# Row pairs in flight and attention weight pieces kept for both token halves: a change to a two-block transformer kernel

## The reference, cut to what matters

```python
for i in range(DEPTH):                      # DEPTH = 2
    h = x * scale + shift
    f = short_conv_mixer(h, ...) if i % 2 == 0 else diff_attention(h, w_qkv, ...)
    x = layer_norm(ALPHA * x + gate * f, ...)
    h = x * scale + shift
    f = peer_ffn(h, w_q[i], sub_keys[i], u[i], v[i])
    x = layer_norm(ALPHA * x + gate * f, ...)
```

```python
act = gelu(einsum('td,thkd->thk', xc, u[idx]))
out = einsum('thk,thkd->td', g * act, v[idx])
```

## Time and profile before

| | us |
|---|---|
| runs (3) | median 2861.89, 2859.72 to 2866.51 |
| the profiled execution | 2860.44 |
| its span, first to last instruction | 2858.7 |
| TensorE busy | 2556.7 (89%) |
| VectorE busy | 1577.9 (55%) |
| ScalarE busy | 630.5 (22%) |
| POOL busy | 674.2 (24%) |
| mean rate of the transfers | 329 GB/s |
| mean granted TensorE clock | 0.982 |

### The profile page before, as it was taken

One profiled execution on the slowest core, in us unless ns is written; L12 is line 12 of the kernel. 1 busy time (PEld: TensorE's weight loads), 2 busy tenths in 40 slices (PEclk: granted clock), 3 DMA queues, 4 the chain that ended last, 5 costly groups with the idle time before them and its releaser, 6 DMA issues.

```text
span 2858.7 us, 26727 instructions
## 1 busy us (share of the span) xinstructions
PE 2556.7 (89%) x9887; PEld 1591.7 (56%) x9887; DVE 1577.9 (55%) x3459; ACT 630.5 (22%) x1826; POOL 674.2 (24%) x687
## 2 busy tenths in 40 slices
PE   7999989999999899999889877999878999777776
PEld 6874548856884578758555422655525646322222
DVE  4562135524551546533768885365795565974544
ACT  1001211001000120000223333342333533332222
POOL 1110000100010001100234454243353243544332
PEclk9999999999999999999999999999999999999999
DMA  9894426845793448856789999999999999999997
GB/s 384 343 362 152 186 79 258 352 180 199 294 356 119 191 170 335 314 189 261 273 340 421 421 421 421 418 413 421 420 420 399 411 422 421 421 410 421 421 421 313
DMA packets 121128, 941.46 MB, mean 329 GB/s; under 512 B 14845, under 2 KB 16277, under 8 KB 19494
## 3 DMA queue, kind: packets, MB, share of 16 engines
q0 software_dynamic: 93344, 669.09, 57.8%
q1 hardware_dynamic: 27654, 270.66, 24.0%
HBM read 938.65 MB, written 1.05 MB: 329 GB/s over the span
## 4 chain that ended last, share of the span: by engine, by line
PE 62%; DMA 22%; DVE 9%; ACT 3%; issue 1%; SPq 1%; POOL 1%; DVEq 0%; POOLq 0%
PE psW L917 19%; DMA ring<-in_peer_uv_dram,lamt 19%; PE psF L1257 11%; PE psF L856 11%; DVE ring L2439 4%; PE psW L1358 3%; DMA mring<-in_tail_w_dram 2%; PE psW L826 2%; PE psW L796 2%; PE psW L1276 2%; PE psW L785 2%; PE psF L892 1%; POOL ring L630 1%; PE psF L1173 1%; PE psW L837 1%
## 5 line engine op out<-in xcount | busy, mean ns | idle before, releaser
L1257 PE MATMUL psF<-ring,p_diag 128*128 128x512 f32 x2048 | 959.5, 614 | 226.9 <-ACT p_diag L1663 226.6
L2439 DVE SCALAR_TENSOR_TENSOR ring<-ring,h 128x1024 f32<-128x1024 f32 x512 | 620.8, 1224 | 435.3 <-DMA ring<-in_peer_uv_dram,lamt 432.0
L630 POOL DMA_INDIRECT ring<-in_peer_uv_dram,lamt x512 | 585.4, 1143 | 1017.2 <-PE psF L1257 819.6
L1257 PEld LDWEIGHTS psF<-ring,p_diag 128*128 128x128 f32 x2048 | 380.6, 194 | 749.2 <-issue 391.4
L917 PE MATMUL psW<-hT,ring 128*128 128x256 f32 x2560 | 558.4, 380 | 1.9 <-DMA ring<-in_gu_t_dram 1.9
L917 PEld LDWEIGHTS psW<-hT,ring 128*128 128x128 f32 x2560 | 487.3, 190 | 77.5 <-issue 10.0
L856 PE MATMUL psF<-ring,arena 128*128 128x512 f32 x704 | 304.2, 593 | 3.2 <-DVE arena L2098 3.0
L856 PEld LDWEIGHTS psF<-ring,arena 128*128 128x128 f32 x704 | 133.4, 190 | 171.7 <-issue 166.5
L1656 ACT ACTIVATE small<-small 128x2 f32<-128x2 f32 x256 | 52.0, 203 | 698.2 <-DVE ring L2439 698.0
L1663 ACT ACTIVATE p_diag<-ident,small 128x128 f32<-128x128 f32 x512 | 177.6, 394 | 8.4
L1544 ACT ACTIVATE arena<-psW 128x256 f32<-128x256 f32 x88 | 33.8, 384 | 602.6 <-PE psW L917 543.7
(11 more groups left out here) (314 smaller groups left out, 2212.6 us busy)
## 6 DMA issues: line engine op xcount, KB each, us to landing
ring<-in_gu_t_dram SPq DMA_DIRECT2D x44, 2048.0 KB, 8.7
mring<-in_tail_w_dram SPq DMA_DIRECT2D x56, 1024.0 KB, 9.1
mring<-in_mod_t_dram POOLq DMA_DIRECT2D x43, 1024.0 KB, 7.3
ring<-in_down_t_dram SPq DMA_DIRECT2D x20, 2048.0 KB, 9.0
mring<-in_row_t_dram POOLq DMA_DIRECT2D x39, 1024.0 KB, 7.2
ring<-in_conv_in_t_dram SPq DMA_DIRECT2D x12, 2048.0 KB, 7.5
M<-in_mod_t_dram POOLq DMA_DIRECT2D x21, 1024.0 KB, 7.0
M<-in_row_t_dram POOLq DMA_DIRECT2D x19, 1024.0 KB, 7.6
```

Source lines behind the costliest of these rows:

```text
L630: pool.indirect_dma_start(out=pair(n % PAIRS), out_offset=None, in_=rows, in_offset=bass.IndirectOffsetOnAxis(ap=s_idx[:, c:c + 1], axis=0 ...
L1257: ins = pe.matmul(psF[:, b, f * HALF:(f + 1) * HALF], p_diag[:, n % PAIRS, :], row_v(n % PAIRS)[:, f * HALF:(f + 1) * HALF], start=(i == 0 ...
L2439: dve.scalar_tensor_tensor(row_u(c), row_u(c), 1.0, h[:, b, :], ALU.mult, ALU.mult, accum_out=p_dots[:, c:c + 1]).then_inc(dot_done, 1)
```

## The change

PAIRS goes from 8 to 6. The ring place that held slots 6 and 7 no longer holds row pairs. The value pieces of the attention (the first KEPT = 4 of the 24) get homes of their own: two are in that ring place (`left`), one in `arena[:, 4096:6144]`, one in the first 2048 columns of `M[:, 0]`. Each of the four has its own semaphore, is loaded once, and is read by both `attend(0)` and `attend(1)`. All other pieces still alternate between the two `mring` places; `passed(n)` counts them without the kept ones. A kept piece waits for nothing that was used in `mring`, only for the ninth unit of `a_full` and for the last output weights of the conv stage. `p_diag` keeps eight columns of matrices, since its memory is also used for a condition row at the start.

```diff
-PAIRS = 8
+PAIRS = 6
+KEPT = 4
...
-    chunk_loaded = [sem(f"chunk_loaded{i}") for i in range(2)]
+    chunk_loaded = [sem(f"chunk_loaded{i}") for i in range(2 + KEPT)]
...
+    left = ring[:, conv7.w % RING, :]
+    chunk_homes = [mring[:, 0].rearrange("p k n -> p (k n)"), mring[:, 1].rearrange("p k n -> p (k n)"),
+                   arena[:, 4096:6144], M[:, 0, 0:2].rearrange("p v n -> p (v n)"), left[:, 0:2048], left[:, 2048:4096]]
+
+    def kept(n):
+
+        return n >= FIRST_CHUNKS and (n - FIRST_CHUNKS) % CHUNKS < KEPT
+
+    def passed(n):
+
+        return n if n < FIRST_CHUNKS else n - KEPT * ((n - FIRST_CHUNKS) // CHUNKS + 1)
+
+    def chunk_home(n):
+
+        return 2 + (n - FIRST_CHUNKS) % CHUNKS if kept(n) else passed(n) % 2
+
+    def chunk_count(n):
+
+        return 1 if kept(n) else passed(n) // 2 + 1
...
-        home = (conv7.w + (2, 1, 3, 0)[s // 2]) % RING
+        home = (conv7.w + (2, 1, 3)[s // 2]) % RING
...
         def chunk(n, c):
-            if n >= 2:
+            if kept(n):
+                sp.wait_ge(a_full, LAST_QUERY[0] + 1)
+                sp.wait_ge(w_used, outputs[conv7.w + 8])
+            elif n >= 2:
                 done = n - 2 - FIRST_CHUNKS
+                if kept(n - 1) or kept(n - 2):
+                    done -= KEPT
                 if done < 0:
-                    sp.wait_ge(a_full, LAST_QUERY[n - 2] + 1)
+                    sp.wait_ge(a_full, LAST_QUERY[done + FIRST_CHUNKS] + 1)
...
-            sp.dma_start(mring[:, n % 2].rearrange("p k n -> p (k n)"), a["tail_w_2"][c]).then_inc(chunk_loaded[n % 2], 16)
+            sp.dma_start(chunk_homes[chunk_home(n)], a["tail_w_2"][c]).then_inc(chunk_loaded[chunk_home(n)], 16)
...
-                chunk(FIRST_CHUNKS + CHUNKS * b + c, FIRST_CHUNKS + c)
+                if b == 0 or not kept(FIRST_CHUNKS + c):
+                    chunk(FIRST_CHUNKS + CHUNKS * b + c, FIRST_CHUNKS + c)
...
-            elif n in (4, 6):
-                pool.wait_ge(w_used, outputs[conv7.w + 7 + (n - 4) // 2])
+            elif n == 4:
+                pool.wait_ge(w_used, outputs[conv7.w + 7])
...
-            pe.wait_ge(chunk_loaded[i % 2], 16 * (i // 2 + 1))
-            return mring[:, i % 2].rearrange("p k n -> p (k n)")
+            pe.wait_ge(chunk_loaded[chunk_home(i)], 16 * chunk_count(i))
+            return chunk_homes[chunk_home(i)]
```

More of the change, by code:

```diff
@@ L220, in _program @@
     p_w = small[:, 112:112 + PAIRS]
-    p_diag = sb("p_diag", [P, PAIRS, P])
+    p_diag = sb("p_diag", [P, 8, P])
     given_cols = arena[:, 14080:14296]
```

## The result

| | before | after |
|---|---|---|
| median of the runs, us | 2863.6 (4 runs) | 2923.3 (4 runs, 2905.2 to 2935.0) |
| ratio, 95% interval | | 1.020 (1.018 to 1.023) |
| profiled execution, us | 2860.4 | 2905.2 |
| its span, us | 2858.7 | 2903.5 |

The change makes the kernel **2.0% slower, 60 us**, where 19 us were forecast. The sign was right and the size was not. The profiled execution of the changed kernel is the fastest of its four: it lost 45 us, and the other three 14 to 30 us more, with a mean granted clock that falls from 0.979 to 0.965 as the time rises.

A forecast was written before the change was run, and what follows sets the result against it. The prediction took the tail, from the start of the row transfers, to be bound by bytes. Its terms, 0.0 + 5.0 + 1.7 + 10.0 + 3 = +19.7 us, gave 2881 us, with 8 in 10 between 2854 and 2900.

The forecast's parts named there:

- (1): In the tail, four value pieces are loaded once, not per token half: -10.0 us if the engines stay busy.
- (5): Value steps: TensorE becomes the bound; its gains and the moved loads' +10.0 us in the first pass net 0.0 us.
- (3): Start of the row transfers: the stock is emptied, +5.0 us, and VectorE's seventh and eighth row come +1.7 us late.
- (4): Ends of second and third pass: VectorE drains the last expert choice, the stock is empty both times, +10.0 us.
- (2): Pure stretches: six slots leave 7.7 us for a landing, 5.7 is the least, so the engines' pace holds.
- (6): Three stretches elsewhere and two places where VectorE normalises a block: thin stock costs +3 us, bounds 0 and 12.
- A: Whole tail: bytes decide, depth does not; six slots keep engines as busy as eight, 2852 us; chance 0.15.
- B: A draw: idle time at start and ends is real, but extra pieces fill idle engines; 2867 or 2863; chance 0.17.
- C: Pure stretches: the loop of six does not close, steps take 5.3 us, 25 us on top: 2906; chance 0.12.

The follow-up runs named there:

- experiment 1: Kernel before, with six slots and nothing kept: 1.0195; seven slots: 1.0038; nine: 0.9996; eight with two value pieces kept: 1.0000.
- the second trace: The changed kernel run and profiled again, nothing altered: 2919.9 us, ratio 1.0192.
- experiment 6: No kept pieces, ScalarE working row by row instead of by steps, against the kernel before: five slots 1.0351, six 1.0074, seven 1.0003.
- five (by rows): Five slots, no kept pieces, ScalarE handling each row as soon as its dot product is there, against the kernel before: 1.0351.
- experiment 2: Changed kernel with the four kept pieces loaded at their old times, not in a row behind piece 7: 2916.0 us, 1.0175.
- experiment 5: One idle TensorE product per step in the fourth and later first pass: changed kernel 2924.2 us, 1.0210; kernel before 2869.5 us, 1.0020.

## Why the prediction was right or wrong

**What bounds the kernel**: right, and the experiments sharpen it. Transfers bound the tail so long as the queue is deep enough, and eight slots is where that begins.

**(1), (5) Fewer bytes and the value steps**: the mechanism was right, sizes a little off. The page of the changed kernel has 4.2 MB less on SP's queue. Row pairs 48 to 64 cost 11.6 us (10.0 forecast for the burst; by experiment 1 about 8 are the burst's and 4 depth's). The value stretches gained 19.1 (14.3), and the waits for feature pieces went. The value steps themselves are as long as before, 6.89 us, as said: TensorE is the bound there. Behind them, where the forecast put 1.0 and 3.3 us, 1.5 and 6.5 were lost, and as much with nothing kept. So the term that the forecast netted at 0.0 is 11.6 - 19.1 + 8.0 = +0.5 us in the trace. Six slots without kept pieces cost the same as with them (1.0195, and 1.0203 and 1.0192), within some 10 us.

**(3) The start**: +8.0 us in place of +6.7. In 1460 to 1500 the share went from 0.90 to 0.84.

**(4) The ends of the second and third pass**: +15.2 in place of +10.0, and +15.2 again in the second trace. With seven slots it is +4.4, so the loss goes with the slots. The sign that the forecast named, a lower DMA share, came at the end of the third pass (0.95, 0.97 before) and not at that of the second (0.97, 0.92 before; 377 GB/s against 375), so the share did not show what the time shows. The clock reads 0.91 in both stretches (0.95 and 0.94 before), which the forecast did not include; no run tells its cost there.

**(2) The loop of six**: this is the first step that failed. It said "So a pure stretch still runs at the engines' pace, with 2.0 us in hand in place of 7.0". Most steps do run at 4.97 us, and the first landing of a step is then 7.7 us. But now and then one comes late, by 0.2 to 1.6 us, and the mean of the 54 steps is 5.12 us; a pure step longer than 4.97 us was the forecast's own sign that (2) is wrong. VectorE's dot products in the changed kernel:

```profile
2678.02 1.22 DVE L2466 SCALAR_TENSOR_TENSOR ring<-ring,h 128x1024 f32<-128x1024 f32 x1 [1.26 <-DMA ring<-in_peer_uv_dram,lamt]
2680.50 1.22 DVE L2466 SCALAR_TENSOR_TENSOR ring<-ring,h 128x1024 f32<-128x1024 f32 x1 [1.25 <-DMA ring<-in_peer_uv_dram,lamt]
2683.82 1.23 DVE L2466 SCALAR_TENSOR_TENSOR ring<-ring,h 128x1024 f32<-128x1024 f32 x1 [2.08 <-DMA ring<-in_peer_uv_dram,lamt]
...
2686.14 1.23 DVE L2466 SCALAR_TENSOR_TENSOR ring<-ring,h 128x1024 f32<-128x1024 f32 x1 [1.09 <-DMA ring<-in_peer_uv_dram,lamt]
```

The third is 3.32 us behind the second in place of 2.49, though its transfer was issued in time (2675.28). It took 8.5 us to land, and the loop leaves 7.7; what made it late is not known. That the time is then not won back is what the length of the pass says. Of the 54 steps of rows 400 to 508, 15 are longer than 5.1 us in the changed kernel, 1 before, none with seven slots. The shortest landing of the whole program, 5.7 us, was the wrong floor: with 7.7 us left for a landing the fourth pass loses 3 to 7 us, in the execution with the clock's cycle 17; with 10.2 us left it loses nothing. Where between the two the need lies, no run shows.

**(6) Thin stock elsewhere**: the step that failed by the most. Of the +30.0 us of "everything else", 8.0 lie behind the value steps and 7.2 in the fourth pass. The other 15 or so stand against "I take **+3 us**"; in the second trace they are 22, with six slots and nothing kept 25. The test was the wrong one. It took the shortest landing under eight slots, less 5.0 us, against 5.7, and so looked only at what is travelling. In a stretch with VectorE busy 84 of 95 us steps are long and short in turn, and by the explanation of experiment 6, which is argued, what counts is how many row pairs can wait, landed, for a short step. I had a number that should have warned, landings from 10.4 to 15.8 us in 2040 to 2135 in place of the even 12.0 to 13.5 of the earlier trace rows.

**What remains of the miss.** By passes the trace has +24, +4, +5 and +12.5 us, where the forecast had 17 for the first and next to nothing for the second and third. The sum by places is the fastest execution's, 2905.2 us. The median of the four is 18 us above it. The second trace (2916.8 us) puts 2 us of such a difference at the start and 5 in "everything else"; the mean clock was lower, and what the rest is stays open.

**Rivals.** A (2852 us) and B (2867, 2863): both excluded by depth's own price of some 55 us. C, "the loop of six does not close", came nearest: 2906 against 2923, in part by luck. Its place, the pure stretches, was only partly right (it put 25 us there, and the fourth pass lost 7.2), and its test, "it decides once no landing comes under 7.7 us", was wrong: landings down to 5.5 us are still there. The Trainium skill (Trainium Kernel Development and Optimization, Best Practices) says "Double-buffer for performance: Overlap DMA with compute". It gives no number of slots for a queue like this one; here five (by rows), six, seven and eight slots measured 1.035, 1.0195, 1.004 and 1.

**The numbers**: the range ended at 2900, 23 us short. Its upper end priced (6) at 12 us by four stretches of 2 to 3 us, that is by the same wrong test that gave the middle. A range around a term must come from another way to price it, not from more of the same one.

## What to carry to other kernels

Before taking a buffer from a ring that keeps the DMA engines full, count three things: the loop without waiting, a margin for late landings (here 7.7 us for a landing were too few and 10.2 enough), and the row pairs that must lie ready while the consumer is away for a long step. The last is argued here, not shown; uneven steps and a wide spread of the landing times are the signs to look for. Saved bytes are worth little where another engine becomes the bound as soon as they are gone, and little beside the depth that they cost: 10 us of transfers saved here, 60 us lost. Shortening the time from landing to release is worth nearly as much as a buffer (34 us here for some 2.7 us, against 44 for the seventh slot) and costs no memory. It is worth less where the loop has room: 10 us with seven slots (1.0038 to 1.0003), 4 with eight.

## What the runs showed of the hardware

- A DMA share of 1.00 with 408 GB/s in place of 421 (2600 to 2880 above). The typical packet is no slower: in rows 400 to 508 the median time of an 8 KiB packet is 0.309 us in the changed kernel and 0.313 before. But 1.6% of them take over 0.5 us, where 0.06% did before, and that lifts the mean from 0.314 to 0.320 us. Six slots with nothing kept have 0.8% of such packets and 416 GB/s there, the execution of experiment 2 has 2.5% and 395. Whether the long packets cost the time or only show an engine that waits is open. The share counts them as busy, so the GB/s column is the one to compare.
- In one execution TensorE's waits of 2.9 to 3.5 us were each followed by products at the lower granted clock, and waits of 1.1 us between them were not; the pattern came back every 16.8 us (experiment 5). That the slow products themselves bring the next wait, through slots that come back late, is argued; it fits that with the waits cut in two the clock stayed at 1.00.
- The changed kernel's executions scattered over 30 us in the first four (2905 to 2935) and over 12 in four others; the kernel before scattered over 7 us in four and over 17 in 27, six slots with nothing kept over 10 in four. So six slots may scatter more, but few executions say so. What differs between the longer and the shorter ones, beyond the lower mean clock of the longer in the first four, is open.
